# Modulation weights issued together, small loads moved to the GpSimd queue, and the first tile's modulation moved to ScalarE in a hybrid layer kernel

## The chip, the cores and the metric

The kernel runs on one core of one Trainium2 chip. The metric is the device time of one execution in microseconds. The engines are PE (TensorE), DVE (VectorE), ACT (ScalarE), POOL (GpSimd) and SP (SyncE); each has its own program, and they wait for each other through semaphores. Transfers are issued from the queue of SP, ACT or POOL, and 16 DMA engines carry them out.

## The reference

One layer over 256 tokens of width 1024, all in f32, and a final norm:

```
mod = silu(c) @ w_ada + b_ada          # six vectors of 1024
h   = rms_norm(x, g_norm1) * (1 + sc1) + sh1
z   = h @ w_in + b_in                  # 5376 columns: u, v, q, k, v, gates A and B
A   = gmlp_spatial(gelu(u), gelu(v))   # uses w_spatial, b_spatial
B   = sliding-window attention(q, k, v) with rotary (positions) and sinks
x   = x + gt1 * ((sig(gA) * (A @ w_o_a) + sig(gB) * (B @ w_o_b)) @ w_out)
x   = x + gt2 * MoE(rms_norm(x, g_norm2) * (1 + sc2) + sh2)   # top 4 of 32 experts
out = rms_norm(x, g_final)
```

## The kernel before, in words

The tokens are two tiles of 128 (t = 0, 1). The weights of the dense part come in 17 blocks of up to 512 columns (v0, v1, u0, u1, q0, q1, kv, ga0, ga1, gb0, gb1, then oa, ob, out in two each), those of the modulation in 12 blocks of 512 columns (ada0 to ada11). A block of either kind has 2 MB. Four buffers hold them: ring 0 to 2 hold ada1, ada2 and ada3 first and then the dense blocks in turn, ring 3 holds ada0 and then ada4 to ada11. A load waits until the block before it in its buffer has been used (`item_used`, in `load` at L385).

A dense block is computed in three passes of eight matmuls for each tile (`rows_times`, L1242). Both operands are split in an upper part (a cast to fp32r, L741) and a lower part (the difference). The passes are lower h and upper h times the upper weights, and upper h times the lower weights. The upper part of the weights is made by DVE (`w_parts_upper`, L743), the lower part half by DVE (`w_parts_lower`, L751) and half by POOL (L505); both are line L329 in the profile. The third pass of a tile waits for both halves. The parts of h are made by `x_parts` (L762, L765) for each tile.

A modulation block is one group of 16 matmuls on a replicated silu(c) (`ada`, L1269, matmuls L1277), a copy by ACT (`part_copy`, L536, L547), and four small products that add the quarters (`ada_rows`, L1281, L1288). ada0 to ada3 are needed for h: their results and b_ada are added (L810), transposed (L1319) and give the columns `mod_col` and `mul1` (L813, L815). ada4 to ada11 are spread between the dense blocks.

The order of the work is written out by hand, one program for each engine; nothing else decides it.

- SP (L379): c, x; then it waits for ACT's small loads (`cond_in`, L383); ada0 to ada3 (L402); v0, after ada1 is used, and its bias; the small loads w_spatial, b_spatial, positions, four of sinks, w_router, b_router (L407 to L416) and four of b_ada (L417, issued at L375); ada4, v1, u0, and from there one modulation block, one dense block and one bias at a time. After the dense part the weights of the experts, in 20 slots.
- ACT (L530): the small loads g_norm1 and four of b_ada; silu(c) (L554); the squares of x (L558), a square root (L561), the copies of ada0 to ada3; h of tile 1 (L571); then the loads of the layer norm's gain and bias (L577) and the gelus (L583).
- DVE (L730): the replicated silu(c), the inverse root (L777 to L785), the normalised x (L806); L810 to L815; h of tile 0 (L823); x_parts of tile 0, w_parts_upper of v0, x_parts of tile 1, w_parts_lower of v0, then v1.
- POOL (L482): constants until L497; it waits for w_spatial and b_spatial (L500), clears the masked part of w_spatial (L501), and then makes its half of each block's lower part in turn (L505).
- PE (L1217): 16 transposes of the normalised x (L1309), ada0 to ada3 (L1314), the transposes of the modulation (L1319), v0 of both tiles, ada4, the transposes of w_spatial (L1336), v1 and so on (L1321).

DVE waits for positions and sinks (L859) after the bias of v0, and for the rest of b_ada (L873) before the bias of v1. The experts' part (L1540 to L1641) goes through 32 experts with blocks of 32 tokens; its gate and up products are L1592, its down products L1627.

The lines of the pass that the steps speak of are

```
for n, (lhsT, w) in enumerate(((up, w_upper[i % 2]), (low, w_upper[i % 2]), (up, w_lower[i % RING]))):
    if n == 2:
        pe.wait_ge(ev("w_lower_dve"), i + 1)
        pe.wait_ge(ev("w_lower_pool"), i + 1)
```

Of the kernel before, what the change touches and what calls it, by code (L numbers as in the profile page):

```python
# [11 lines left out]
ALU = mybir.AluOpType  # L12
ACT = mybir.ActivationFunctionType
AX = mybir.AxisListType

P = 128
# [45 lines left out]
def bass_hybrid_layer(nc, x, c, positions, w_ada, b_ada, g_norm1, w_in, b_in, ln_v_g, ln_v_b,  # L62
# [47 lines left out]
    with ctx:  # L110
# [269 lines left out]
        def _(sp):  # L380
            sp.dma_start(c_col, c[0].rearrange("(k p) -> p k", p=P)).then_inc(c_in, 16)
            sp.dma_start(x_sb[:, :, :], x[0].rearrange("(t p) d -> p t d", p=P)).then_inc(x_in, 16)
            sp.wait_ge(cond_in, 80)  # L383

            def load(name, w, used=None):  # L385
                if used:
                    item_used(sp, used)
                slot = ring_slot(name)[0]
                sp.dma_start(ring[slot][:, :, 0:w.shape[1]],
                             w.rearrange("(k p) n -> p k n", p=P)).then_inc(ring_in[slot], 16)  # L390

            def load_ada(j, used=None):
                load(f"ada{j}", w_ada[0, :, j * COLS:(j + 1) * COLS], used)
# [8 lines left out]
            for j in range(4):  # L402
                load_ada(j)
            load(*dense[0][:2], "ada1")
            load_bias(0)

            sp.dma_start(ws, w_spatial[0].rearrange("h i j -> i h j")).then_inc(gmlp_in, 16)  # L407
            sp.dma_start(bs, b_spatial[0].rearrange("h i -> i h")).then_inc(gmlp_in, 16)
            sp.dma_start(pos_i[:, :], positions[0].rearrange("(t p) -> p t", p=P)).then_inc(attn_in, 16)
            for hh in range(2):  # L410
                for r in range(2):
                    sp.dma_start(sk[hh * CH:(hh + 1) * CH, r, :],
                                  sinks[0:1, :].rearrange("a (g m) -> a m g", m=4)[:, 2 * hh + r, :].to_broadcast([CH, 4]))\
                       .then_inc(attn_in, 16)
            sp.dma_start(wr, w_router[0].rearrange("(k p) e -> p k e", p=P)).then_inc(route_in, 16)
            sp.dma_start(br, b_router[0:1, :].to_broadcast([P, E])).then_inc(route_in, 16)  # L416
            load_b_ada(sp, 4, 12, b_ada_in)  # L417
            load_ada(4, "ada0")
# [64 lines left out]
        def _(pool):  # L483
# [15 lines left out]

            pool.wait_ge(gmlp_in, 32)  # L500
# [30 lines left out]
        def _(act):  # L531
# [34 lines left out]
            for h in range(2):  # L566
                name = f"xT1{h}"
                bank = z_wait(act, name)
                for i in range(4):
                    k = 4 * h + i  # L570
                    last = act.activation(hT[:, k, P:2 * P], bank[:, i * P:(i + 1) * P], ACT.Identity,  # L571
                                          bias=mod_col[:, 0, k:k + 1], scale=mul1[:, k:k + 1])
                z_done(last, name)
# [157 lines left out]
        def _(dve):  # L731
# [85 lines left out]
            dve.wait_ge(ev("mod_col_ready"), 2)  # L817
            for h in range(2):
                name = f"xT0{h}"
                bank = z_wait(dve, name)  # L820
                for i in range(4):
                    k = 4 * h + i
                    last = dve.tensor_scalar(hT[:, k, 0:P], bank[:, i * P:(i + 1) * P], mul1[:, k:k + 1],  # L823
                                             mod_col[:, 0, k:k + 1], ALU.mult, ALU.add)
                z_done(last, name)
            for t in range(TILES):
                for h in range(2):
                    z_gone(dve, f"xT{t}{h}")
                x_parts(hT, upper_a, hT_lower, "hT_parts", slice(t * P, (t + 1) * P))
                if t == 0:  # L830
                    w_parts_upper(0)
            w_parts_lower(0)
# [833 lines left out]
```

## Time and profile before

| | |
|---|---|
| median of 3 runs | 1365.93 us (1364.82 to 1366.85) |
| the profiled execution's own time | 1366.62 us |
| its span in the profile | 1364.6 us |
| PE, DVE, ACT, POOL busy | 80%, 31%, 16%, 9% |
| mean granted clock of PE | 0.878 of 2.4 GHz |
| moved by DMA | 473.22 MB, mean 347 GB/s |

The profile shows one execution. Busy times are of the engines' own instructions; SP and the queues (SPq, ACTq, POOLq) show how long issuing a transfer took, which is not how long the transfer lasted. L12 is line 12 of the kernel. A line can be a helper's: L389 issues every weight block, L741 every cast to an upper part, L329 every lower part of weights. "idle before" is the time that the engine stood still just before an instruction, and behind the arrow is what ended it.

### The profile page before, as it was taken

What the parts mean: (1) busy time and instruction counts of PE and PEld (TensorE: products, weight loads), DVE (VectorE), ACT (ScalarE), POOL (GpSimd) and SP (SyncE); (2) the same over time, 40 slices, a digit from 0 to 9 for tenths busy, and PEclk for the clock granted to TensorE, in tenths of its full rate; (3) what the DMA queues carried; (4) which work ended last, traced back from release to release, by engine and by line L of the source; (5) the groups of instructions that cost most, each with busy time, mean ns of one, the idle gap of its engine ahead of it and who ended that gap; (6) DMA issues with size and microseconds to landing.
All of it is one profiled execution on the core that took longest, in us unless ns stands there. A gap on an engine that the chain in (4) does not pass through costs nothing.

```text
span 1364.6 us, 26032 instructions
## 1 busy us (share of the span) xinstructions
PE 1096.6 (80%) x10234; PEld 508.0 (37%) x10235; DVE 425.8 (31%) x990; ACT 222.4 (16%) x428; POOL 117.9 (9%) x46
## 2 busy tenths in 40 slices
PE   3689999986997668756899989998667687967874
PEld 1457677864332223111343434343211133311322
DVE  1487687965221112111222222222111122211214
ACT  2112123023211011000111212121100011100112
POOL 0154344510000000000000000000000000000001
PEclk9699999985997779768899989999787788977978
DMA  8786965629999999999869999829999996999991
GB/s 308 249 318 234 356 231 177 218 88 384 416 416 416 415 417 418 417 417 416 366 252 417 418 392 371 367 107 418 416 418 417 418 393 264 417 417 416 415 416 44
DMA packets 113244, 473.22 MB, mean 347 GB/s; under 512 B 12784, under 2 KB 16496, under 8 KB 80272
## 3 DMA queue, kind: packets, MB, share of 16 engines
q1 hardware_dynamic: 110880, 469.03, 86.0%
q10 hardware_dynamic: 2288, 3.02, 0.8%
q8 instruction: 67, 1.10, 0.3%
q14 instruction: 9, 0.07, 0.0%
HBM read 470.98 MB, written 1.05 MB: 346 GB/s over the span
## 4 chain that ended last, share of the span: by engine, by line
PE 36%; SPq 26%; DMA 26%; DVE 5%; issue 5%; ACT 1%; POOL 0%; ACTq 0%; DVEq 0%
PE bank L1592 13%; SPq L360 12%; SPq L354 11%; DMA gate_up<-in_w_down_dram 10%; DMA gate_up<-in_w_gate_up_dram 9%; PE bank L1255 9%; PE bank L1627 6%; DMA down<-in_w_down_dram 3%; DVE gate_up_r L741 2%; PE bank L1558 2%; PE bank L1544 2%; DMA gate_up<-in_w_in_dram 1%; DMA gate_up<-in_w_o_b_dram 1%; DMA gate_up<-in_w_ada_dram 1%; PE bank L1277 1%
## 5 line engine op out<-in xcount | busy, mean ns | idle before, releaser
L1592 PE MATMUL bank<-gate_up,mod 128*32 128x512 f32 x2592 | 362.2, 684 | 118.1 <-DMA gate_up<-in_w_gate_up_dram 73.4
L1186 DVE TENSOR_SCALAR front<-bank 128x256 f32<-128x256 f32 x50 | 21.2, 424 | 709.4 <-PE bank L1592 709.4
L1592 PEld LDWEIGHTS bank<-gate_up,mod 128*32 128x32 f32 x2592 | 78.9, 118 | 332.9 <-issue 165.9
L1627 PE MATMUL bank<-gate_up,mod 128*32 128x256 f32 x2496 | 152.6, 389 | 35.2 <-DMA gate_up<-in_w_down_dram 31.2
L1255 PE MATMUL bank<-gate_up_r 128*128 128x512 f32 (+1 forms) x544 | 138.2, 401 | 20.1 <-DVE gate_up_r L741 11.3
L1255 PEld LDWEIGHTS bank<-gate_up_r 128*128 128x128 f32 x544 | 101.7, 194 | 49.2 <-issue 20.8
L329 POOL TENSOR_TENSOR gate_up_r<-gate_up,gate_up_r 128x2048 fp32r<-128x2048 f32 (+1 forms) x17 | 108.8, 6398 | 128.3 <-DVE gate_up_r L741 128.3
L1592 PE MATMUL bank<-down,mod 128*32 128x512 f32 x608 | 91.3, 716 | 27.5 <-DMA down<-in_w_gate_up_dram 25.2
L1627 PEld LDWEIGHTS bank<-gate_up,mod 128*32 128x32 f32 x2496 | 75.2, 111 | 101.0 <-DMA gate_up<-in_w_down_dram 46.1
L712 ACT ACTIVATE front<-front 128x256 f32<-128x256 f32 x50 | 20.8, 416 | 537.7 <-DVE front L1186 537.7
L526 POOL TENSOR_TENSOR gate_up<-x_sb,gate_up 128x1024 f32<-128x1024 f32 x2 | 4.7, 2352 | 1038.2 <-DVE x_sb L1209 1038.2
L1558 PE MATMUL bank<-front 32*128 32x256 f32 x816 | 67.7, 452 | 0.5 <-ACT front L724 0.5
L1255 PE MATMUL bank<-gate_up_r,down_r 128*128 128x512 f32 (+1 forms) x272 | 67.5, 391 | 0.0
L712 ACT ACT_TABLE_LOAD x50 | 64.2, 1283 | 1.4 <-issue 0.5
L1558 PEld LDWEIGHTS bank<-front 32*128 32x128 f32 x816 | 42.3, 213 | 55.3 <-issue 51.8
L1544 PE MATMUL bank<-h,front 128*32 128x256 f32 x816 | 57.5, 401 | 1.3 <-DVE front L1130 1.3
L724 ACT ACTIVATE front<-bank 128x256 f32<-128x256 f32 x50 | 19.2, 384 | 225.9 <-PE bank L1627 225.9
L1255 PEld LDWEIGHTS bank<-gate_up_r,down_r 128*128 128x128 f32 x272 | 51.9, 194 | 11.1
L1627 PE MATMUL bank<-down,mod 128*32 128x256 f32 x704 | 42.8, 387 | 13.1 <-DMA down<-in_w_down_dram 12.3
L1592 PEld LDWEIGHTS bank<-down,mod 128*32 128x32 f32 x608 | 17.9, 119 | 87.4 <-DMA down<-in_w_gate_up_dram 59.6
L741 DVE CAST gate_up_r<-gate_up 128x4096 fp32r<-128x4096 f32 (+1 forms) x17 | 43.0, 2530 | 15.9 <-DMA gate_up<-in_w_in_dram 15.7
L1125 DVE TENSOR_SCALAR front<-front 128x2 f32 (+1 forms) x101 | 23.0, 229 | 76.5 <-issue 75.3
(254 smaller groups left out, 829.2 us busy)
## 6 DMA issues: line engine op xcount, KB each, us to landing
gate_up<-in_w_gate_up_dram SPq DMA_DIRECT2D x204, 1024.0 KB, 20.8
gate_up<-in_w_down_dram SPq DMA_DIRECT2D x104, 1024.0 KB, 23.1
down<-in_w_gate_up_dram SPq DMA_DIRECT2D x52, 1024.0 KB, 20.9
gate_up<-in_w_ada_dram SPq DMA_DIRECT2D x12, 2048.0 KB, 9.0
down<-in_w_down_dram SPq DMA_DIRECT2D x24, 1024.0 KB, 24.6
gate_up<-in_w_in_dram SPq DMA_DIRECT2D x10, 2048.0 KB, 14.5
gate_up<-in_w_o_a_dram SPq DMA_DIRECT2D x2, 2048.0 KB, 7.7
gate_up<-in_w_o_b_dram SPq DMA_DIRECT2D x2, 2048.0 KB, 10.5
```

Of the source, the lines that this page charges most:

```text
L329: return eng.tensor_tensor(w_lower[i % RING][:, chunks, 0:cols], ring[i % RING][:, chunks, 0:cols], w_upper[i % 2][:, chunks, 0:cols], ALU ...
L354: eng.dma_start(store(at % SLOTS), w_gu_view[:, bass.ds(e, 1), k, :].rearrange("p a n -> p (a n)"))\
L360: eng.dma_start(store(at % SLOTS).rearrange("p (a n) -> p a n", a=2), w_dn_view[:, bass.ds(e, 1), 2 * i:2 * i + 2, :].rearrange("p a k n - ...
L712: act.activation(g_sig, g_cap, ACT.Sigmoid, scale=ALPHA).then_inc(ev("sig_ready"), 1)
L741: return dve.tensor_copy(dst, src)
L1125: return dve.tensor_scalar(slots, slots_gates[:, bass.ds(e, 1), 0:2].rearrange("p a t -> p (a t)"), slot_base[:, bass.ds(g, 1)], None, ALU ...
L1186: dve.tensor_scalar(g_cap, banks[4][:, 0:HW], LIMIT, None, ALU.min).then_inc(ev("g_ready"), 1)
L1255: last = pe.matmul(bank[:, 0:cols], lhsT[:, k, rows], w[:, k, 0:cols], start=(n == 0 and k == 0), stop=(n == 2 and k == KC - 1))
L1544: last = pe.matmul(banks[6][q * BM:(q + 1) * BM, 0:HW], sel[:, t, :], h2[:, t, q * HW:(q + 1) * HW], start=(t == 0), stop=(t == 1), skip_g ...
L1558: last = pe.matmul(banks[q][:, t * HW:(t + 1) * HW], gT[rows, t * P:(t + 1) * P], y_sb[rows, :], start=False, stop=True, skip_group_check= ...
L1592: last = pe.matmul(banks[4][q * BM:(q + 1) * BM, :], xT[:, k % KG, k // KG, :], w[:, :, q * HW:(q + 1) * HW], start=(k == 0), stop=(k == K ...
L1627: last = pe.matmul(banks[7][q * BM:(q + 1) * BM, 0:HW], hidT[:, k % KG, k // KG, :], w[:, k % 2, q * HW:(q + 1) * HW], start=(k == 0), sto ...
```

## The change

SP issues x after ada0 and ada1, and ada2 and ada3 behind it; its wait for ACT's small loads is gone. The small loads L407 to L417 go from SP's queue to POOL's, which issues them after its constants, with w_spatial, b_spatial and b_ada first. SP's ada4 comes ahead of v0's bias. ACT makes h of both tiles; DVE makes the upper part of v0's weights meanwhile, and the lower part between the parts of tile 0 and those of tile 1.

```diff
@@ sync
             sp.dma_start(c_col, c[0].rearrange("(k p) -> p k", p=P)).then_inc(c_in, 16)
-            sp.dma_start(x_sb[:, :, :], x[0].rearrange("(t p) d -> p t d", p=P)).then_inc(x_in, 16)
-            sp.wait_ge(cond_in, 80)
...
-            for j in range(4):
+            for j in range(2):
+                load_ada(j)
+            sp.dma_start(x_sb[:, :, :], x[0].rearrange("(t p) d -> p t d", p=P)).then_inc(x_in, 16)
+            for j in range(2, 4):
                 load_ada(j)
             load(*dense[0][:2], "ada1")
+            load_ada(4, "ada0")
             load_bias(0)
-
-            sp.dma_start(ws, w_spatial[0].rearrange("h i j -> i h j")).then_inc(gmlp_in, 16)
-            sp.dma_start(bs, b_spatial[0].rearrange("h i -> i h")).then_inc(gmlp_in, 16)
-            sp.dma_start(pos_i[:, :], positions[0].rearrange("(t p) -> p t", p=P)).then_inc(attn_in, 16)
-            for hh in range(2):
-                for r in range(2):
-                    sp.dma_start(sk[hh * CH:(hh + 1) * CH, r, :],
...
-            sp.dma_start(wr, w_router[0].rearrange("(k p) e -> p k e", p=P)).then_inc(route_in, 16)
-            sp.dma_start(br, b_router[0:1, :].to_broadcast([P, E])).then_inc(route_in, 16)
-            load_b_ada(sp, 4, 12, b_ada_in)
-            load_ada(4, "ada0")
             load(*dense[1][:2], "ada2")
@@ gpsimd, behind the constants
+            pool.dma_start(ws, w_spatial[0].rearrange("h i j -> i h j")).then_inc(gmlp_in, 16)
+            pool.dma_start(bs, b_spatial[0].rearrange("h i -> i h")).then_inc(gmlp_in, 16)
+            load_b_ada(pool, 4, 12, b_ada_in)
+            pool.dma_start(pos_i[:, :], positions[0].rearrange("(t p) -> p t", p=P)).then_inc(attn_in, 16)
+            for hh in range(2):
+                for r in range(2):
+                    pool.dma_start(sk[hh * CH:(hh + 1) * CH, r, :],
...
+            pool.dma_start(wr, w_router[0].rearrange("(k p) e -> p k e", p=P)).then_inc(route_in, 16)
+            pool.dma_start(br, b_router[0:1, :].to_broadcast([P, E])).then_inc(route_in, 16)
+
             pool.wait_ge(gmlp_in, 32)
@@ scalar
-            for h in range(2):
-                name = f"xT1{h}"
...
-                    last = act.activation(hT[:, k, P:2 * P], bank[:, i * P:(i + 1) * P], ACT.Identity,
...
+            for t in range(TILES):
+                for h in range(2):
+                    name = f"xT{t}{h}"
...
+                        last = act.activation(hT[:, k, t * P:(t + 1) * P], bank[:, i * P:(i + 1) * P], ACT.Identity,
...
@@ vector
-            dve.wait_ge(ev("mod_col_ready"), 2)
-            for h in range(2):
-                name = f"xT0{h}"
...
-                    last = dve.tensor_scalar(hT[:, k, 0:P], bank[:, i * P:(i + 1) * P], mul1[:, k:k + 1],
...
+            w_parts_upper(0)
             for t in range(TILES):
                 for h in range(2):
                     z_gone(dve, f"xT{t}{h}")
                 x_parts(hT, upper_a, hT_lower, "hT_parts", slice(t * P, (t + 1) * P))
                 if t == 0:
-                    w_parts_upper(0)
-            w_parts_lower(0)
+                    w_parts_lower(0)
             w_parts_upper(1)
             w_parts_lower(1)
```

## Rows read from the trace of the kernel before

**Rows 1.** By stage: length, busy PE, PEld, DVE, ACT, POOL; clock, DMA share, GB/s.

```profile
78.35:155.00 76.65, 76.32 (x448) 55.64 (x448) 54.10 (x73) 12.88 (x21) 33.49 (x6) 1.00 0.78 275
```

**Rows 2.** The chain of waits up to 90 us: start, us, what.

```profile
54.04 15.11 DMA gate_up<-in_w_in_dram
```

**Rows 3.** SP's timeline (start, us, group): the small loads' first, second and last group.

```profile
29.18 0.44 SPq L407 DMA_DIRECT2D gate_up<-in_w_spatial_dram  x1
29.66 7.61 SPq L408 DMA_DIRECT2D sm<-in_b_spatial_dram  x1
...
44.99 8.51 SPq L375 DMA_DIRECT2D mod<-in_b_ada_dram  x4
```

**Rows 4.** PE's timeline from v0 on; in brackets idle before, and what ended it.

```profile
47.65 3.75 PE L1255 MATMUL bank<-gate_up_r 128*128 128x512 f32 x8 [7.57 <-DVE gate_up_r L741]
...
55.87 5.53 PE L1255 MATMUL bank<-gate_up_r 128*128 128x512 f32 x16 [2.03 <-DVE gate_up_r L329]
...
66.81 1.09 PE L1336 MATMUL bank<-ident,gate_up 128*128 128x128 f32 x8
71.61 2.52 PE L1255 MATMUL bank<-gate_up_r 128*128 128x512 f32 x8 [3.70 <-DVE gate_up_r L741]
...
78.35 2.08 PE L1255 MATMUL bank<-gate_up_r 128*128 128x512 f32 x8 [1.25 <-POOL gate_up_r L329]
...
80.71 2.12 PE L1255 MATMUL bank<-gate_up_r 128*128 128x512 f32 x8
...
86.38 1.92 PE L1277 MATMUL bank<-gate_up,crep 128*32 128x512 f32 x16
```

**Rows 5.** PE's timeline until the modulation is done.

```profile
18.07 2.07 PE L1277 MATMUL bank<-gate_up,crep 128*32 128x512 f32 x16
...
20.87 0.43 PE L1288 MATMUL bank<-gate_up,quarter_head 128*32 128x128 f32 x8 [0.73 <-ACT gate_up L547]
...
27.65 2.69 PE L1277 MATMUL bank<-gate_up,crep 128*32 128x512 f32 x16 [2.35 <-DMA gate_up<-in_w_ada_dram]
...
33.07 3.64 PE L1277 MATMUL bank<-gate_up,crep 128*32 128x512 f32 x16 [1.37 <-DMA gate_up<-in_w_ada_dram]
...
37.43 0.66 PE L1288 MATMUL bank<-gate_up,quarter_head 128*32 128x128 f32 x8 [0.72 <-ACT gate_up L547]
```

**Rows 6.** ACT's timeline at the first square of x.

```profile
8.21 1.06 ACT L558 ACTIVATE down<-x_sb 128x1024 f32<-128x1024 f32 x1 [3.03 <-DMA x_sb<-in_x_dram]
```

**Rows 7.** Two stretches of the modulation, columns as in rows 1.

```profile
24.00:28.50 4.50, 1.43 (x20) 0.44 (x20) 0.00 (x0) 0.60 (x1) 0.00 (x0) 1.00 1.05 386
28.50:38.20 9.70, 6.80 (x44) 1.13 (x36) 0.00 (x0) 1.19 (x2) 0.00 (x0) 0.51 1.05 385
```

**Rows 8.** ACT's DMA queue (q10) from 2 to 8.5 us: packets, MB, share of 16 engines.

```profile
q10 hardware_dynamic: 1616, 0.27, 26.3%
```

**Rows 9.** DVE's timeline from the modulation columns on.

```profile
40.40 0.17 DVE L815 SCALAR_TENSOR_TENSOR sm<-sm 128x8 f32<-128x8 f32 x1
...
43.35 0.69 DVE L741 CAST gate_up_r<-down 128x1024 fp32r<-128x1024 f32 x1
...
45.22 2.29 DVE L741 CAST gate_up_r<-gate_up 128x4096 fp32r<-128x4096 f32 x1
...
48.14 5.47 DVE L765 TENSOR_TENSOR down_r<-down,gate_up_r 128x1024 fp32r<-128x1024 f32 x1
53.53 2.28 DVE L329 TENSOR_TENSOR gate_up_r<-gate_up,gate_up_r 128x2048 fp32r<-128x2048 f32 x1
```

**Rows 10.** Groups of instructions up to 78 us: busy us, mean ns, idle before.

```profile
L571 ACT ACTIVATE down<-bank,sm 128x128 f32<-128x128 f32 x8 | 2.9, 467 | 3.2 <-DVE sm L815 3.2
```

**Rows 11.** POOL's timeline: its wait for the small loads, and v1's half.

```profile
42.56 0.52 POOL L501 MEMSET gate_up<- 64x512 f32 x1 [39.16 <-DMA sm<-in_b_spatial_dram]
...
71.54 6.67 POOL L329 TENSOR_TENSOR gate_up_r<-gate_up,gate_up_r 128x2048 fp32r<-128x2048 f32 x1 [19.01 <-DVE gate_up_r L741]
```

**Rows 12.** The page's DMA issues: count, KB each, median us to landing.

```profile
gate_up<-in_w_o_a_dram SPq DMA_DIRECT2D x2, 2048.0 KB, 7.7
```

More of the change, by code:

```diff
@@ L401, in load_bias @@
                                  dense[i][2].to_broadcast([P, cols])).then_inc(bias_in[i % 2], 16)
-            for j in range(4):
+            for j in range(2):
+                load_ada(j)
+            sp.dma_start(x_sb[:, :, :], x[0].rearrange("(t p) d -> p t d", p=P)).then_inc(x_in, 16)
+            for j in range(2, 4):
                 load_ada(j)
             load(*dense[0][:2], "ada1")
+            load_ada(4, "ada0")
             load_bias(0)
-            sp.dma_start(ws, w_spatial[0].rearrange("h i j -> i h j")).then_inc(gmlp_in, 16)
-            sp.dma_start(bs, b_spatial[0].rearrange("h i -> i h")).then_inc(gmlp_in, 16)
-            sp.dma_start(pos_i[:, :], positions[0].rearrange("(t p) -> p t", p=P)).then_inc(attn_in, 16)
-            for hh in range(2):
-                for r in range(2):
-                    sp.dma_start(sk[hh * CH:(hh + 1) * CH, r, :],
-                                  sinks[0:1, :].rearrange("a (g m) -> a m g", m=4)[:, 2 * hh + r, :].to_broadcast([CH, 4]))\
-                       .then_inc(attn_in, 16)
-            sp.dma_start(wr, w_router[0].rearrange("(k p) e -> p k e", p=P)).then_inc(route_in, 16)
-            sp.dma_start(br, b_router[0:1, :].to_broadcast([P, E])).then_inc(route_in, 16)
-            load_b_ada(sp, 4, 12, b_ada_in)
-            load_ada(4, "ada0")
             load(*dense[1][:2], "ada2")
@@ L498, in _ @@
                                pattern=[[-QR, NQT], [0, P]], channel_multiplier=1).then_inc(ev("consts"), 1)
+            pool.dma_start(ws, w_spatial[0].rearrange("h i j -> i h j")).then_inc(gmlp_in, 16)
[5 more added lines that the diff above has]
+                    pool.dma_start(sk[hh * CH:(hh + 1) * CH, r, :],
+                                   sinks[0:1, :].rearrange("a (g m) -> a m g", m=4)[:, 2 * hh + r, :].to_broadcast([CH, 4]))\
+                        .then_inc(attn_in, 16)
+            pool.dma_start(wr, w_router[0].rearrange("(k p) e -> p k e", p=P)).then_inc(route_in, 16)
+            pool.dma_start(br, b_router[0:1, :].to_broadcast([P, E])).then_inc(route_in, 16)
             pool.wait_ge(gmlp_in, 32)
@@ L565, in _ @@
             act.wait_ge(ev("mod_col_ready"), 2)
-            for h in range(2):
-                name = f"xT1{h}"
-                bank = z_wait(act, name)
-                for i in range(4):
-                    k = 4 * h + i
-                    last = act.activation(hT[:, k, P:2 * P], bank[:, i * P:(i + 1) * P], ACT.Identity,
-                                          bias=mod_col[:, 0, k:k + 1], scale=mul1[:, k:k + 1])
-                z_done(last, name)
+            for t in range(TILES):
+                for h in range(2):
+                    name = f"xT{t}{h}"
+                    bank = z_wait(act, name)
+                    for i in range(4):
+                        k = 4 * h + i
+                        last = act.activation(hT[:, k, t * P:(t + 1) * P], bank[:, i * P:(i + 1) * P], ACT.Identity,
+                                              bias=mod_col[:, 0, k:k + 1], scale=mul1[:, k:k + 1])
+                    z_done(last, name)
             for t in range(TILES):
@@ L816, in _ @@
                .then_inc(ev("mod_col_ready"), 2)
-            dve.wait_ge(ev("mod_col_ready"), 2)
-            for h in range(2):
-                name = f"xT0{h}"
-                bank = z_wait(dve, name)
-                for i in range(4):
-                    k = 4 * h + i
-                    last = dve.tensor_scalar(hT[:, k, 0:P], bank[:, i * P:(i + 1) * P], mul1[:, k:k + 1],
-                                             mod_col[:, 0, k:k + 1], ALU.mult, ALU.add)
-                z_done(last, name)
+            w_parts_upper(0)
             for t in range(TILES):
```

## The prediction

> **What bounds the kernel now.** The page shows no single bound, so I read the busy time by stage, then the chain of waits of the front, and last each engine's timeline there. From 78 to 155 us PE is busy 76.3 of 76.7 us [rows 1]. What comes after is fixed by data, each load waiting for the use of the buffer before it, so I take all behind 78 us to shift as one block. The change is then read at one event: the start of v1's third pass for tile 0, at 78.35 us now. From there PE runs without a break.
>
> The chain up to it ends in the load of v1, issued at 54.04 and landed at 69.17 [rows 2]. SP could not issue it earlier: it was busy with the twelve small loads from 29.18 to 53.50 us, end to end [rows 3]. PE's timeline shows the price: idle 2.0 us in v0 (for DVE's L329), 3.7 before v1 (for its cast) and 1.25 in it (for POOL) [rows 4]. These 7.0 us can be won behind v0's first matmul, and what matmuls lose after a gap: v1's first pass took 2.52 us, 2.12 the next time.
>
> Ahead of v0 the modulation loads bound. PE waits for ada2 and ada3, which come in 5.42 us apart (27.65, 33.07) [rows 5].
>
> **The change part by part.**
>
> *x behind two modulation loads.* x, now the first large load, has landed at 8.21 us, when ACT's square starts [rows 6]. With ada0 and ada1 ahead of it, 5.42 us each, it lands at 19.1 us at the earliest. This matters, since PE's program has the 16 transposes of the normalised x ahead of ada0: nothing of the modulation is computed before x is there. Early weights gain nothing by themselves.
>
> *The POOL queue's packets.* They now run beside the critical ones. I count 5,504 for the twelve moved loads from their shapes: 1,024 each for w_spatial, b_spatial, the four of b_ada together, the four of sinks and w_router, 256 for positions and 128 for b_router. ACT's small loads had 1,616 packets, for 26.3% of 6.5 us: 1.7 us of all engines [rows 8]; 5,504 would be 5.8 us. How many go ahead of x no row shows: from none (x at 19.1) to all (24.9). No row is nearer to one end, so I take half: x at 22.0.
>
> *To the modulation columns.* From x landed to ada0's matmuls 9.86 us (8.21 to 18.07): squares, root, normalisation, transposes [rows 5, 6]. Then four steps. The last weights land at 30 to 36 us (8.21 and four times 5.42, and the packets) and are used at 41.6, so the steps run back to back: 2.80 from the matmuls to the start of L1288 (18.07 to 20.87) and 0.43, 3.23 each, 12.9 together. From the last L1288's end to L815's end 2.48 (38.09 to 40.57) [rows 5, 9]. Sum: 22.0 + 9.9 + 12.9 + 2.5 = 47.3 us, against 40.6 now: **6.7 us later**. This needs the high clock. The granted clock is 1.00 (2.4 GHz) from 24 to 28.5 us, and 0.51 (near 1.2 GHz) from 28.5 to 38.2; the fall follows a stretch in which PE was busy 1.43 of 4.5 us [rows 7]. Ada0's 16 matmuls took 2.07 us, ada3's 3.64 [rows 5]. Now PE would be busy 2.5 of each 3.23 us, so I expect no fall.
>
> *hT by ACT, DVE at the weights.* Now ACT makes tile 1 and DVE tile 0 side by side; DVE then casts and subtracts tile 0 (1.9 us, 43.35 to 45.22) and casts v0 (2.29), and PE starts at 47.65, 7.1 us after the columns [rows 4, 9]. In the new order DVE casts v0 first while ACT makes tile 0 (2.9 us for eight [rows 10]); tile 1 costs ACT as much again, beside DVE's work. But the cast releases POOL's half of v0's subtraction, and DVE and POOL take turns: beside POOL's half DVE's L765 took 5.47 us, where cast and subtraction together had taken 1.9, and POOL's L329 took 6.67 beside DVE's, which takes 2.28 [rows 9, 11]. So POOL, 4.4 us alone, runs from 2.4 to 6.8 us after the columns, DVE's 1.9 us on hT only then, and PE starts at 8.7 instead of 7.1: **1.6 us lost** where the step was meant to gain.
>
> *The load of v1.* Without the small loads SP issues v0 when ada1 is used, at 37.2 us. A 2 MB load into a free queue lands after 7.7 us [rows 12], at 44.9; DVE wants it at 47.3. ada4, the bias and v1 follow by 56.4; DVE wants v1 at 60.3. Both are covered, by 2.4 and 3.9 us.
>
> *PE from there.* Passes 1 and 2 of v0 6.2 us (47.65 to 53.84); then from the unbroken stretch 1.9 for the third pass, 5.7 for tile 1 (80.71 to 86.38), 1.9 for ada4, 1.1 for L1336 and 3.8 for two passes of v1 [rows 4]: 20.5 us without a wait. DVE has v0's halves ready 11 us after the columns, DVE and POOL v1's by 22; PE asks at 14.9 and 29.2. **Sum:** 47.3 + 8.7 + 20.5 = 76.5 against 78.35, **1.9 us won**. Before it was 40.6 + 7.1 + 30.7. So 10.2 us of idle time and slow matmuls go, and 6.7 and 1.6 come back.
>
> *POOL's twelve issues.* No row shows an issue on POOL. On SP the twelve took 24.3 us, one of them 7.61, one 0.44 [rows 3]; at these two prices each they would take 5.3 and 91. POOL is free from 3.4 us (42.56 less its 39.16 of waiting) [rows 11]; with SP's prices it is done at 27.7, 22 us before its first subtraction. I take that, as the same loads are the nearest rows. The Trainium skill, "DMA: Bandwidth & Descriptors", section "SWDGE vs HWDGE vs iDMA", says that GpSimd's descriptors are computed by software and SP's and ACT's by hardware, and the page gives about 1 us to the first byte against 0.6. An estimate by that ratio makes 40.5 us of issues, done at 43.9, and leaves the sum as it is; no row here shows it.
>
> The loads from POOL have other users: w_spatial's mask, needed by PE at about 73 us; positions and sinks, for DVE behind v0's bias at about 70; the rest of b_ada before v1's bias. At 27.7 us all are early. What POOL's issues delay first is its half of v0.
>
> **Against the runs.** The profiled execution took 1366.6 us, the median of the runs is 1365.93, 0.7 us less. So 1364.7 for it and **1364.0** for the median. With x at either end the gain is 4.8 or -1.0 us: 1361.1 to 1366.9. A measurement can tell 0.2% here, 2.7 us.
>
> **The rivals.**
>
> *A. POOL issues until 50 to 54 us: 1360.2.* Then DVE comes first: hT is cast and subtracted 4.9 us after the columns, PE starts at 52.2, POOL's half is ready before 58.4, and 3.8 us more are won, 5.7 in all. For it: twice SP's price is plausible. Against: the window is narrow.
>
> *B. Slower: POOL still issues when PE wants its half.* The place is POOL's first L329. PE starts as in A and wants it at 58.4, with 5.7 us in hand; the half takes 4.4, so the sign turns when the issues end at 59.7, and beyond it each us costs one. That is 56.3 us for twelve, 4.7 each against SP's mean 2.0. At three times SP's sum (end at 76.3) the loss is 16.6 us: 1382.5. For it: 5,504 packets, most of 4 to 512 bytes, and no row for POOL. Against: SP's issues waited in part for a full queue, so their price alone is lower. The Trainium skill, "SBUF — State Buffer", section "SBUF: two separate sides", says that a two-port DVE instruction keeps GpSimd from writing descriptors. By that page DVE's work before ada0 would be added to POOL's issues: at most the 14.7 us between 3.4 and 18.07, an end at 42.4, so alone it decides nothing.
>
> *C. Slower: the modulation runs at the low clock.* Then each of the four steps takes 3.64 + 0.72 + 0.66 = 5.0 us, 7.2 more in all, and 5.3 us are lost: 1371.2. For it: PE now stands idle until 28 us. Against: ada0's matmuls came behind the same transposes and ran in 2.07 us [rows 5].
>
> *D. The change doesn't do what it says*: x isn't held back by the weights ahead of it. If it shared the engines with ada0 alone it would land at 13.6 us, the columns would be there at 38.9 instead of 47.3, still behind all weights, and 10.3 us were won: 1355.6. Against: ada2 and ada3, on one queue, landed strictly one after the other [rows 5].
>
> **Chances.** Forecast case 0.55, of which 0.38 within 0.2%, 0.14 faster and 0.03 slower (its own range 1361 to 1367); A 0.15, B 0.14, C 0.10, D 0.06. B and C are slower but for 0.02 within 0.2%. Faster 0.14 + 0.15 + 0.06 = 0.35; slower 0.03 + 0.22 = 0.25; same 0.38 + 0.02 = 0.40. The range goes from A (1360.2, with 0.7 for the spread of the runs) to C's 1371.2, as 1359.5 to 1371.5; outside are most of B and D.
>
> **What would show it.** Right: ACT's first square at 19 to 25 us; the four L1277 groups at 1.9 to 2.1 us each without a DMA wait; L815 near 47; the first L1255 near 56, after POOL's L329; the third pass of v1 near 76.5 with PE unbroken from v0; no SP issues from 24 to 37 us. Wrong if: POOL's last issue ends after 50 us; x lands before 19 us; PE's clock is 0.5 during the modulation; PE waits for v1 or u0 all the same; or the stretches behind 78 us change their lengths by over 2 us.

## The result and the profile after

The changed kernel takes 1378.83 us, the median of 4 runs (1377.42 to 1380.06), beside 1365.66 for the kernel before: a ratio of 1.0100 as recorded, 95% interval 1.0084 to 1.0115 (the quotient of these two medians is 1.0096). It is **1% slower**, 14.8 us above the forecast and 7.3 above the range. The profiled execution has a span of 1378.1 us, 13.5 more than before.

The small loads that change queues are thirteen, not twelve as the prediction and the expectations have it: w_spatial, b_spatial, positions, four of sinks, w_router, b_router and four of b_ada.

The timeline of the front, all engines (start, us, group; in brackets the idle time before and what ended it):

```profile
3.35 1.11 POOL L489 DMA_DIRECT2D gate_up<-in_w_spatial_dram  x1
...
11.13 20.23 SPq L387 DMA_DIRECT2D gate_up<-in_w_ada_dram  x2
...
11.71 0.59 POOL L499 DMA_DIRECT2D sm<-in_b_router_dram  x1
...
35.38 1.06 ACT L559 ACTIVATE down<-x_sb 128x1024 f32<-128x1024 f32 x1 [30.29 <-DMA x_sb<-in_x_dram]
...
45.24 2.79 PE L1270 MATMUL bank<-gate_up,crep 128*32 128x512 f32 x16
...
57.34 0.43 PE L1281 MATMUL bank<-gate_up,quarter_head 128*32 128x128 f32 x8 [0.72 <-ACT gate_up L548]
...
59.62 0.17 DVE L817 SCALAR_TENSOR_TENSOR sm<-sm 128x8 f32<-128x8 f32 x1
...
62.08 4.50 POOL L329 TENSOR_TENSOR gate_up_r<-gate_up,gate_up_r 128x2048 fp32r<-128x2048 f32 x1 [48.38 <-DVE gate_up_r L743]
62.83 4.30 DVE L743 CAST gate_up_r<-down 128x1024 fp32r<-128x1024 f32 x1 [0.83 <-ACT down L573]
...
67.16 1.22 DVE L767 TENSOR_TENSOR down_r<-down,gate_up_r 128x1024 fp32r<-128x1024 f32 x1
...
68.44 3.78 PE L1248 MATMUL bank<-gate_up_r 128*128 128x512 f32 x8 [9.14 <-DVE down_r L767]
...
88.73 1.98 PE L1248 MATMUL bank<-gate_up_r 128*128 128x512 f32 x8
```

The row to see is ACT's: x has landed at 35.38 us, where it had landed at 8.21 [rows 6]. Everything behind hangs on it. PE has 16 transposes of x ahead of ada0, so its first ada0 matmul comes at 45.24 (18.07 before, [rows 5]), the columns at 59.8 instead of 40.6 [rows 9], v0 at 68.44 instead of 47.65, and v1's third pass at 88.73 instead of 78.35 [rows 4]. From there on the stage is the old one:

Three stretches of after: from v1's third pass on, from the logits to the first expert, and the experts (length, busy PE, PEld, DVE, ACT, POOL; clock, DMA share, GB/s).

```profile
88.73:165.40 76.67, 76.18 (x449) 55.55 (x447) 48.10 (x71) 13.10 (x21) 30.68 (x6) 1.00 0.81 288
327.43:360.69 33.26, 27.78 (x162) 15.38 (x166) 13.03 (x62) 10.23 (x13) 0.00 (x0) 0.60 1.02 414
360.69:1378.10 1017.41, 802.60 (x8640) 296.12 (x8632) 199.31 (x667) 145.04 (x256) 4.69 (x2) 0.87 0.92 376
```

The first stands against [rows 1]: 76.67 us and 76.65. The logits' first matmul comes 10.9 us later than before (327.43 against 316.57). So 10.9 of the 13.5 us are lost in the front. The other two stretches took 34.63 and 1013.40 us before: 1.4 us are won and 4.0 lost, so 2.6 more are lost, the 4.0 of them some 290 us and more behind the last changed line's work. These splits come from one execution of each kernel. Two later kernels with the same front (h1 and h2, below) have the logits at 324.4 and 324.5 us, so the front's loss is 8 to 11 us.

The page of after, DMA queues (packets, MB, share of 16 engines):

```profile
q1 hardware_dynamic: 105168, 467.83, 84.8%
q10 hardware_dynamic: 2288, 3.02, 0.8%
q0 software_dynamic: 608, 1.21, 0.7%
q8 instruction: 67, 1.10, 0.3%
q14 instruction: 34, 0.28, 0.1%
```

q1 is SP's queue, q10 ACT's, q0 is new and POOL's. q14, which carries instructions, had 9 packets before and has 34; what that means is told with h1 to h3.

What delayed x, in the DMA queues of three windows of after: 3 to 35.4 us (q1, q0), 14 to 20 (q0, q1), and 24 to 35.4 (q1).

```profile
q1 hardware_dynamic: 3409, 7.32, 64.9%
q0 software_dynamic: 608, 1.21, 27.7%
...
q0 software_dynamic: 217, 0.23, 51.2%
q1 hardware_dynamic: 217, 0.41, 31.3%
...
q1 hardware_dynamic: 1872, 4.28, 97.1%
```

From 14 to 20 us the engines carry one packet of q0 for each of q1: 217 and 217. Those of q0 take 51.2% of 96 engine microseconds, 0.23 us each; the q1 stream, 0.387 MB/us when alone (2 MB in 5.42 us), falls to 0.07. The Trainium skill, "DMA: Bandwidth & Descriptors", section "Queues, rings and completion order", says that each DMA engine goes round between the queues that have work, a whole packet at a time; the equal counts agree. Over the front q0's 608 packets take 27.7% of 32.4 us, 9.0 us of all engines. And q1 had moved 7.32 MB when x was complete, though x ends at 5.24 MB of its queue (two blocks and 1 MB). The engines were out of step: some were at ada2 and ada3 while the slowest still owed its part of x. 2.08 MB at 0.387 are 5.4 us. 9.0 and 5.4 are 14.4 of the 15.9 us by which x was later than in e1, below.

This is an account, not the whole mechanism. For some microseconds the engines did not even work at their full share (columns as in rows 1):

```profile
17.00:18.00 1.00, 0.00 (x0) 0.00 (x0) 0.00 (x0) 0.00 (x0) 0.00 (x0) 1.00 0.48 33
18.00:19.00 1.00, 0.00 (x0) 0.00 (x0) 0.00 (x0) 0.00 (x0) 0.00 (x0) 1.00 0.71 17
19.00:20.00 1.00, 0.00 (x0) 0.00 (x0) 0.00 (x0) 0.00 (x0) 0.00 (x0) 1.00 0.45 52
```

From 17 to 20 us they were busy 48, 71 and 45% and moved 33, 17 and 52 GB/s, although x was still owed. From 18 to 19 us 11 packets of q0 took 65.4% of the 16 engines' time, almost the whole microsecond each. Why the idle engines were not at q1's stream no run shows; SP stood in its issue of ada2 and ada3 at that time (11.13 to 31.36 us).

### The profile page after: what moved, and what is told of

Its sections match the earlier page's. It is cut to its first block, busy times and chain, and to the rows that moved or that the text cites. A ratio compares the mean times of both kernels' runs of the same rounds, so it can differ in the third digit from the quotient of the medians.

```text
span 1378.1 us, 26031 instructions
## 1 busy us (share of the span) xinstructions
PE 1087.2 (79%) x10234; PEld 504.6 (37%) x10235; DVE 418.9 (30%) x982; ACT 225.5 (16%) x436; POOL 126.5 (9%) x59
## 3 DMA queue, kind: packets, MB, share of 16 engines
q1 hardware_dynamic: 105168, 467.83, 84.8%
q10 hardware_dynamic: 2288, 3.02, 0.8%
HBM read 470.98 MB, written 1.05 MB: 343 GB/s over the span
## 4 chain that ended last, share of the span: by engine, by line
PE 37%; DMA 27%; SPq 22%; issue 7%; DVE 5%; ACT 2%; ACTq 0%; DVEq 0%
PE bank L1585 13%; DMA gate_up<-in_w_down_dram 11%; SPq L360 10%; PE bank L1248 10%; SPq L354 10%; DMA gate_up<-in_w_gate_up_dram 9%; PE bank L1620 6%; DMA down<-in_w_down_dram 4%; DMA x_sb<-in_x_dram 2%; DVE gate_up_r L743 2%; PE bank L1551 1%; PE bank L1537 1%; PE bank L1270 1%; DMA gate_up<-in_w_o_b_dram 1%; SPq L349 1%
## 5 line engine op out<-in xcount | busy, mean ns | idle before, releaser
L1620 PE MATMUL bank<-gate_up,mod 128*32 128x256 f32 x2496 | 153.7, 390 | 40.3 <-DMA gate_up<-in_w_down_dram 36.5
L1620 PEld LDWEIGHTS bank<-gate_up,mod 128*32 128x32 f32 x2496 | 75.0, 111 | 106.7 <-DMA gate_up<-in_w_down_dram 52.5
L714 ACT ACT_TABLE_LOAD x50 | 64.2, 1283 | 1.5 <-issue 0.5
L1248 PEld LDWEIGHTS bank<-gate_up_r,down_r 128*128 128x128 f32 x272 | 51.6, 194 | 10.9
L1118 DVE TENSOR_SCALAR front<-front 128x2 f32 (+1 forms) x101 | 23.0, 228 | 76.5 <-issue 75.3
## 6 DMA issues: line engine op xcount, KB each, us to landing
gate_up<-in_w_o_b_dram SPq DMA_DIRECT2D x2, 2048.0 KB, 10.5
```

Of the source, the lines that this page charges most:

```text
L714: act.activation(g_sig, g_cap, ACT.Sigmoid, scale=ALPHA).then_inc(ev("sig_ready"), 1)
L1118: return dve.tensor_scalar(slots, slots_gates[:, bass.ds(e, 1), 0:2].rearrange("p a t -> p (a t)"), slot_base[:, bass.ds(g, 1)], None, ALU ...
L1248: last = pe.matmul(bank[:, 0:cols], lhsT[:, k, rows], w[:, k, 0:cols], start=(n == 0 and k == 0), stop=(n == 2 and k == KC - 1))
L1620: last = pe.matmul(banks[7][q * BM:(q + 1) * BM, 0:HW], hidT[:, k % KG, k // KG, :], w[:, k % 2, q * HW:(q + 1) * HW], start=(k == 0), sto ...
```

## The experiments

Theory L: the packets of POOL's queue delay x, and all else follows as forecast. Its rival X: x would be late anyway behind two blocks, or something else holds the front. (The expectations of e1 and e2 call L "theory P" and the rival Q; in those of g1 to g4 P is another theory, told there.) The table has, in us, x landed, the columns ready, v0's first matmul, v1's third pass, the logits' first matmul, the time from there to the end of the span; then q14's packets, the place of SP's loop in its program (the number of its first instruction; what it is for is told with h1 to h3), the median and its ratio to before with its 95% interval. All times but the last two columns are from one profiled execution of each kernel: after, h1 and h2 have the same front, and x landed at 35.4, 34.1 and 33.9, so a difference of 1.5 us in x, or of 3 us at the logits, says nothing.

| kernel | x | columns | v0 | v1, 3rd | logits | to end | q14 | loop | median | ratio |
|---|---|---|---|---|---|---|---|---|---|---|
| before | 8.2 | 40.6 | 47.7 | 78.4 | 316.6 | 1048.0 | 9 | 84 | 1365.66 | |
| after | 35.4 | 59.8 | 68.4 | 88.7 | 327.4 | 1050.7 | 34 | 71 | 1378.83 | 1.0100 [1.0084, 1.0115] |
| e1 | 19.5 | 44.2 | 49.2 | 86.2 | 325.6 | 1048.4 | 8 | 84 | 1374.3 | 1.0063 [1.0046, 1.0080] |
| e2 | 19.4 | 52.5 | 61.1 | 80.0 | 318.0 | 1053.2 | 34 | 71 | 1373.13 | 1.0065 [1.0048, 1.0081] |
| e3 | 25.0 | 49.5 | 58.1 | 81.5 | 321.3 | 1054.9 | 33 | 76 | 1374.77 | 1.0069 [1.0052, 1.0085] |
| e4 | 28.2 | 51.7 | 56.8 | 84.3 | 322.7 | 1051.4 | 33 | 79 | 1376.91 | 1.0088 [1.0072, 1.0105] |
| e5 | 8.6 | 51.7 | 60.5 | 80.4 | 318.9 | 1051.2 | 34 | 71 | 1371.29 | 1.0055 [1.0038, 1.0071] |
| e6 | 8.3 | 40.0 | 49.5 | 76.9 | 316.6 | 1048.2 | 9 | 84 | 1365.33 | 1.0005 [0.9990, 1.0021] |
| f1 | 8.1 | 38.0 | 45.1 | 68.8 | 307.3 | 1050.0 | 35 | 71 | 1360.14 | 0.9972 [0.9962, 0.9983] |
| f2 | 8.2 | 36.9 | 42.0 | 64.3 | 308.1 | 1051.2 | 34 | 71 | 1361.54 | 0.9978 [0.9965, 0.9991] |
| g1 | 8.2 | 35.7 | 42.8 | 64.9 | 306.1 | 1050.9 | 34 | 71 | 1359.94 | 0.9968 [0.9958, 0.9978] |
| g2 | 8.0 | 40.3 | 47.4 | 77.6 | 316.3 | 1046.5 | 9 | 82 | 1365.07 | 1.0006 [0.9989, 1.0023] |
| g3 | 8.1 | 37.2 | 44.3 | 66.4 | 314.2 | 1047.0 | 9 | 84 | 1363.82 | 0.9996 [0.9983, 1.0009] |
| g4 | 8.0 | 37.0 | 42.0 | 62.6 | 310.2 | 1050.5 | 33 | 71 | 1363.62 | 0.9994 [0.9984, 1.0004] |
| h1 | 34.1 | 57.5 | 66.2 | 85.9 | 324.4 | 1048.2 | 9 | 84 | 1375.3 | 1.0082 [1.0064, 1.0100] |
| h2 | 33.9 | 57.5 | 66.1 | 86.0 | 324.5 | 1050.2 | 34 | 78 | 1378.07 | 1.0103 [1.0085, 1.0121] |
| h3 | 8.0 | 38.0 | 45.1 | 68.8 | 307.1 | 1046.1 | 9 | 84 | 1355.97 | 0.9941 [0.9920, 0.9962] |

**e1: the small loads back on SP**, behind v0's bias, the rest as changed.

```diff
@@ sync, behind load_bias(0); the same lines are taken from gpsimd
+            sp.dma_start(ws, w_spatial[0].rearrange("h i j -> i h j")).then_inc(gmlp_in, 16)
...
+            sp.dma_start(br, b_router[0:1, :].to_broadcast([P, E])).then_inc(route_in, 16)
```

> The changed kernel with its twelve small loads back on SP's queue, behind v0's bias; x stays behind ada0 and ada1, and the new order of hT stays. Theory P (POOL's packets hold x back): x lands at 19 to 20 us instead of 35.4, the modulation columns are there at 43.6, PE starts v0 near 52; SP's small loads then delay v1 again, issued at 55 to 60 us, so the third pass of v1 comes at 78 to 84 and the time is 1366 to 1372 us. Rival Q (the SP queue itself holds x back: its issue took 8.4 us behind two weight blocks, and POOL has no part in it): x lands at 33 us or later and the time is 1377 us or more.

x lands at 19.52 us. That is the 19.1 of two blocks in a row, so L stands and X falls: the two blocks cost 11.3 us, the other 15.9 are POOL's packets. But the gain goes again, and the third pass (78 to 84 expected) and the time (1366 to 1372) both came out later than I had expected: SP issues the small loads from 37.7 to 59.3 us, and POOL, which stands at its wait for b_spatial, can't touch v0's half until 55.86, and v1 is late as well. The line of POOL's timeline:

```profile
55.86 0.52 POOL L502 MEMSET gate_up<- 64x512 f32 x1 [52.47 <-DMA sm<-in_b_spatial_dram]
```

**e2: POOL waits for x** before it issues.

```diff
+            pool.wait_ge(x_in, 16)
             pool.dma_start(ws, w_spatial[0].rearrange("h i j -> i h j")).then_inc(gmlp_in, 16)
```

> The changed kernel, POOL issues its small loads only after x has landed. Theory P: x at 19 to 20 us; POOL's packets then run beside ada2 and ada3. If they cost these what they cost x, ada3 lands near 44, the columns are there at 49 and the time is 1365; if little, columns at 43.6 and 1360. Rival Q: x at 33 us or later, 1377 or more.

x lands at 19.38, but the packets now meet ada2 and ada3 (PE's timeline):

```profile
44.97 3.64 PE L1271 MATMUL bank<-gate_up,crep 128*32 128x512 f32 x16 [6.48 <-DMA gate_up<-in_w_ada_dram]
```

ada3 comes where I had it if the packets cost it what they had cost x (45.0, expected 44), but the time is 8 us above the 1365 expected for that.

**e3 and e4: which of the thirteen.** e3 gives positions and sinks to SP and leaves eight on POOL; e4 leaves those five alone on POOL and gives SP the eight.

```diff
@@ e3: sync (e4: the other eight loads instead)
+            sp.dma_start(pos_i[:, :], positions[0].rearrange("(t p) -> p t", p=P)).then_inc(attn_in, 16)
+            for hh in range(2):
...
```

> The changed kernel with positions and the four loads of sinks on SP behind v0's bias; w_spatial, b_spatial, b_ada, w_router and b_router stay on POOL. Theory P1 (among POOL's packets it is those of the sinks, single 4-byte elements, that block the engines from 16 to 24 us): x lands at 22 to 25 us, 1362 to 1367. Rival P2 (all of POOL's packets cost alike, by bytes or by packets): x lands at 30 us or later, 1373 or more.

> The other half: only positions and sinks on POOL, the rest on SP behind v0's bias. P1: x at 27 us or later. P2: x at 20 to 22 us. The time says less here, since SP's loads delay v1 as well: 1368 to 1378 by P1, 1365 to 1370 by P2.

Against e1's 19.5 the eight delay x by 5.5 us, the five by 8.6, and all thirteen by 15.9. The five move 5 KB: what counts isn't bytes. Nor is it the number of packets: 160 of the 608 are theirs. The trace gives 4 bytes as the size of the elements that they write; b_spatial, one of the eight, is of that kind too, and no run moves it alone. So x came as P1 had it in both, and e4's time too (1376.9, 1368 to 1378 expected), but not e3's (1374.8, 1362 to 1367 expected).

**e5: x first**, the rest as changed.

```diff
+            sp.dma_start(x_sb[:, :, :], x[0].rearrange("(t p) d -> p t d", p=P)).then_inc(x_in, 16)
             def load(name, w, used=None):
```

> The changed kernel with x issued ahead of ada0 again, its one edit; POOL still issues its loads from 3.4 us on. What e1 to e4 left open is whether x's place costs anything of its own, or whether POOL's packets merely delay whichever load is last. Theory L (POOL's packets cost the queue beside them some 16 us, whatever stands there): x lands at 9 to 13 us, but ada3 lands at 43 to 46 (the last of the 9.4 MB landed at 45 in the changed kernel), PE waits for it, the columns are there at 49 to 52 and the third pass of v1 comes at 78 to 82: 1365 to 1372 us. Rival X (only x's place matters): the columns at 37 to 40, the third pass near 68, 1355 to 1358.

x lands at 8.6, and ada0, now the next in the queue, pays:

```profile
28.80 3.20 PE L1270 MATMUL bank<-gate_up,crep 128*32 128x512 f32 x16 [9.91 <-DMA gate_up<-in_w_ada_dram]
```

ada0's matmuls come 10.7 us later than before (18.07), ada3's 11.9 (44.98 against 33.07). So whatever SP's queue holds is delayed, and x's place chooses what. But x's place has a price of its own, too. The columns are ready at 35.7 to 38.0 us with x first and no packets beside it (f1, g1, g3, h3, below), at 44.2 with x behind two blocks (e1), at 51.7 with the packets (e5) and at 59.8 with both (after): 6 to 9 us for x's place, 13 to 16 for the packets, if after's columns are taken at 57.5 (h1) to 59.8.

**e6: the new order of h alone**, on the kernel before (the scalar and vector parts of the diff).

> The kernel before with only the new order of hT (ACT makes both tiles, DVE casts v0 first and makes its lower part between the tiles). By the reading of turns between DVE and POOL: columns at 40.6 as before, PE starts v0 at 49.2 instead of 47.6, its third pass follows without a wait, v1 still comes at 69.2 and hides both, so the third pass of v1 stays at 78.4 and the time at 1364.3 within 2 us. Rival (ACT helps DVE as intended): PE starts at 45.5.

PE starts v0 9.5 us behind the columns instead of 7.1 (8.6 expected), as DVE and POOL take turns at v0's weights. The end doesn't move (1.0005): 2.4 us lost ahead of v0 lie within what PE idled behind it [rows 4].

**f1: what seemed right to do instead.** The kernel before without SP's wait for the conditions and with ada4 ahead of v0's bias; POOL issues the thirteen only behind its half of v0, at 49.9 us, when nothing urgent is in SP's queue.

```diff
@@ gpsimd, behind the constants
+            pool.wait_ge(ev("w_upper_ready"), 1)
+            lower(pool, 0, slice(KC // 2, KC)).then_inc(ev("w_lower_pool"), 1)
+            pool.dma_start(ws, w_spatial[0].rearrange("h i j -> i h j")).then_inc(gmlp_in, 16)
...
+            pool.dma_start(br, b_router[0:1, :].to_broadcast([P, E])).then_inc(route_in, 16)
```

> The kernel before with SP free of the small loads and of its wait for ACT's, and POOL issuing the twelve only behind its first half of a subtraction (v0's). x first, hT as before. Theory P/L: no packet of POOL runs beside the modulation weights; ada3 lands near 30, columns at 37.4, v1 lands near 47 to 52, PE runs v0 and v1 without a wait for a load; third pass of v1 at 67 to 70: 1353 to 1357 us. If instead POOL's packets hold v1 back by the 16 us, third pass at 75 to 80 and 1360 to 1366.

The first version faster than before. v1's third pass comes 9.5 us earlier, the logits 9.2, yet the median wins 4.3, less than the 7 to 11 expected. 2.0 us of that go behind the logits; the rest is the spread of the runs, as the profiled execution of before (1366.62) was 2.2 us above the median of before beside f1 (1364.43), and f1's own 1.05 below its median. **f2** adds the new order of h, with POOL's half of v0 held until the first parts of h stand (`pool.wait_ge(ev("hT_parts"), 1)`):

> As f1 but with the new order of hT, and POOL's first subtraction waits until DVE has made the parts of hT's tile 0, so that POOL can't take its turn ahead of them. By the reading of turns PE starts v0 5 us after the columns instead of 7.1 or 8.7, and v1's third pass comes 26 us after them: near 63.5, 1349 to 1353 us. If the turns are no matter, it is as f1.

PE starts 5.0 us behind the columns, as expected, and loses it again at a modulation block that POOL's packets delay (3.23 us at 75.66); 1361.54 us stand against 1349 to 1353 expected.

**g1 to g4: who issues.** By then kernels with DMAs of POOL's took 1.6 us or more longer behind the logits than the three without. Theory P: using the software queue costs that. Theory N: it doesn't matter who issues; a kernel that comes to the logits earlier waits longer behind them, and the gain goes. g1 is f1 with the thirteen on ACT, g2 the kernel before with the router's two on POOL, g3 is f1 with the thirteen on SP behind v1's bias, g4 is g1 with f2's order.

```diff
@@ g1: scalar, behind its waits for v0's xT
+            act.dma_start(ws, w_spatial[0].rearrange("h i j -> i h j")).then_inc(gmlp_in, 16)
...
+            load_b_ada(act, 4, 12, b_ada_in)
@@ g2: gpsimd, in its loop over the blocks
+                if i == 0:
+                    pool.dma_start(wr, w_router[0].rearrange("(k p) e -> p k e", p=P)).then_inc(route_in, 16)
+                    pool.dma_start(br, b_router[0:1, :].to_broadcast([P, E])).then_inc(route_in, 16)
```

> The order of f1 (x ahead of everything, the weights of the modulation behind it without a wait, the old order of hT), but the twelve small loads are issued by ACT: ten behind its waits for v0's xT and ahead of its layer norm's loads, the router's two behind the copies of block 4; POOL issues no DMA at all. Theory P (a kernel whose POOL issues any DMA loses some 4 us in the expert stage): v1's third pass at 67 to 71 us as in f1 (68.84), logits at 306 to 309, expert stage 1012 to 1013.5 instead of f1's 1015.3, total 1355 to 1357.5. Theory N (the expert stage doesn't care who issued what 900 us earlier; its 4 us are the earlier phase of the stream against its compute): the same front, the expert stage as in f1, total 1359 to 1361. Price of ACT's twelve issues: if they cost as on SP, ACT is 6 us or more late for v0's gelu, v1's third pass at 73 to 76 and total 1361 to 1364.

> The kernel before, with the router's two small loads alone issued by POOL behind its part of the first operator, where nothing in the front waits for them. The front should stand as before: columns ready at 40.6 us, v1's third pass at 78.4, logits at 316.6. Theory P (any DMA issued by POOL costs the expert stage some 4 us): logits unchanged and the total at 1367 to 1369. Theory N (the expert stage depends on the phase in which it starts, not on POOL's queue): 1363.5 to 1365.5.

> f1 without a DMA of POOL's and without one of ACT's: the twelve small loads stay on SP, now behind v1's bias and ahead of u0. SP's 24 us of issues lie behind everything that v0 and v1 need. Front: columns ready at 38, v0 at 45, v1's third pass at 68 to 72. Theory P: expert stage 1011 to 1013, total 1355 to 1358. Theory N: 1359 to 1361. Rival: SP's 24 us of issues now delay u0 and w_in's later blocks, so that logits come at 312 or later and the total at 1362 or more.

> g1 with the new order of hT and POOL's first operator held until the first half of hT stands, as in f2. In f2 PE began v0 5.0 us after the columns instead of 7.1, but POOL's packets delayed the modulation's sixth block. Without these packets: columns at 37 to 38, v0 at 42 to 43, v1's third pass at 63 to 66, logits at 303 to 306. Theory P: total 1352 to 1356. Theory N: the gain of the front is lost again in the expert stage, total 1359 to 1361.

P falls from both sides: g1 has no q0 and takes 1050.9 us to the end, g2 has q0 and takes 1046.5. N gives the right totals for g1 and g2, but not the whole: g1 and g3 are 8 us apart at the logits and still 3.9 at the end. That an early start costs a part stays possible with these four; g1, f1 and h3, below, settle it: logits at 306.1, 307.3 and 307.1, and 1050.9, 1050.0 and 1046.1 us from there. g3's SP is late with the modulation blocks (PE waits 7.42 us for one at 81.86); in g4 ACT issues until 64.2 us and PE waits 2.72 for its copy, so its logits come at 310.2, where I had expected 303 to 306. But the column q14 parts the kernels without an exception: 8 or 9 packets and at most 1048.4 us to the end, or 33 to 35 and at least 1050.0. And it goes with SP's program: the kernels with the 34 packets have at least five loads fewer on SP ahead of its loop over the experts, whichever queue has them.

**h1 to h3: the place of SP's loop.** The loop has six turns, and in the traces of all kernels SP takes 272 instructions from one jump back to the next. Theory I: where it begins decides whether its instructions have to be fetched again in every turn. h1 is the changed kernel with 13 wait instructions more on SP, all long fulfilled, so that the loop begins where it did before; h2, its control, has 7; h3 is g1 with 13. The edit is that of h1 (two waits of the source make one instruction); h2 has `range(13)`.

```diff
             item_used(sp, "ob1")
+            for _ in range(25):
+                sp.wait_ge(x_in, 16)
             first_loads(ring_slots("ob1"))
```

> The changed kernel with 13 wait instructions more on SP, all long fulfilled (on x), between the front's loads and the first loads of the experts. SP's loop over the experts then begins at its 84th instruction, as in the kernel before, instead of its 71st. Theory I (the place of SP's loop decides whether its code stays loaded or is fetched again in every turn): q14 falls from 34 packets to 8 or 9, SP's stretches of issue of 3.2 us go, the front stays as in the changed kernel (x 35.4, v1's third pass 88.7, logits 327.4), expert stage 1012 to 1015 instead of 1017.3, total 1374.5 to 1377. Theory N (the phase in which the stream meets the compute decides, the fetches are harmless): q14 may fall, the total stays at 1378.8 +- 1.

> The control of h1: only 7 wait instructions more, so that SP's loop begins at its 78th instruction, where it was within one of its place in e4 (79), which still had 33 packets on q14. Theory I: q14 at 33 or 34, total as the changed kernel, 1378.8 +- 1. If the wait instructions themselves changed the time, h2 would show half of what h1 shows.

> g1, the fastest so far (1359.94), with the same 13 wait instructions, SP's loop at its 84th instruction. Theory I: q14 8 or 9 packets, front as g1 (v1's third pass 65.0, logits 306.2), expert stage 1012 to 1014.5 instead of 1017.4, total 1355.5 to 1358. Theory N: 1360 +- 1.

h1 and h2 have the same front within 0.15 us. The windows of the experts' stage, h1 and then h2:

```profile
357.49:1372.60 1015.11, 807.41 (x8640) 297.36 (x8632) 199.41 (x667) 145.05 (x256) 4.69 (x2) 0.87 0.92 377
```

```profile
357.61:1374.70 1017.09, 800.17 (x8640) 295.11 (x8632) 199.42 (x667) 145.02 (x256) 4.70 (x2) 0.88 0.92 376
```

and q14 on the pages of h1 and of h2:

```profile
q14 instruction: 9, 0.07, 0.0%
```

```profile
q14 instruction: 34, 0.28, 0.0%
```

Six more instructions, which do nothing, save 2.0 us in this stage and 2.8 in the medians of six runs each (1375.3, 1374.31 to 1377.4, and 1378.07, 1376.6 to 1380.58). In the chain of waits one sees where, in after around 493 us:

```profile
493.66 0.03 SPq L360
493.69 3.18 issue
496.87 0.39 SPq L360
```

SP stands between two loads for 3.18 us and waits for nothing that the profile shows. There are three such stretches of 3.2 us in the experts' part of after (493.69, 645.79, 999.33), three of 4.1 to 4.3 in h2's, none in h1's or h3's, while in all of them SP feeds a stream that keeps the DMA engines busy 92% of the time.

The larger part stands just ahead of them, in the same chain of after:

```profile
638.71 5.57 issue
645.79 3.24 issue
...
992.26 5.55 issue
999.33 3.22 issue
```

At 638.7 and 992.2 us SP has just jumped back to the start of its loop. In the trace's records of SP's own instructions its next one comes 5.1 to 5.8 us behind each of the five jumps back in all ten kernels with 33 to 35 packets, and 0.2 to 0.3 us behind it in the other seven, with 8 or 9. The packets fall into the same places. From 480 to 505 us, around the first jump (486.6), and from 500 to 1350 us after has on q14

```profile
q14 instruction: 4, 0.03, 0.3%
...
q14 instruction: 22, 0.18, 0.1%
```

and h1 has no packet on q14 from 500 to 1350 us. So five jumps cost SP some 27 us in all; most of it is hidden, as SP issues ahead of the stream, and 2 to 3 us are not.

h3 is **the fastest version**: 1355.97 us (1353.6 to 1359.2), 0.6% under the kernel before. Its stretch from the logits is 4.8 us shorter than g1's, more than h1 against h2; with one profile each, how much of that is the fetches isn't settled. Nor is the spread among the kernels with 33 to 35 packets: from 1050.0 (f1) to 1054.9 us (e3) behind the logits, wider than the effect.

## Why the prediction was wrong

**What held.** The bound, in that the event that I chose (v1's third pass) carried the front's part: 10.4 us there, 10.9 at the logits. From x to ada0's matmuls: 9.86 forecast, 9.86 measured. Four steps of the modulation: 12.9 and 12.5 (45.24 to 57.77), at the granted clock of 1.00, so C did not come true. The last L1281's end to the columns: 2.5 and 2.0. v0 8.7 behind the columns: 8.65, for the reason given: beside POOL's 4.50 us DVE's cast took 4.30 instead of 0.69 [rows 9]. From v0 to v1's third pass 20.5: 20.3, without a wait of PE's, though DVE waited 1.99 us for v1, which the forecast had covered by 3.9. POOL's issues: done at 12.3, sooner than the 27.7 taken and than the 43.9 of the estimate beside it; B fell for that reason, and A with it.

**The step that failed** is "The POOL queue's packets": "5,504 would be 5.8 us", and the choice of half of that, "x at 22.0". x came at 35.4. Had it come at 22.0, v1's third pass would have come at 88.73 - 13.4 = 75.3, beside the 76.5 of the sum: this term is the whole error of the front and 1.2 us more, which the other terms gave back. Three things were wrong in it.

- *The price of a packet.* It was taken from ACT's queue [rows 8]: 26.3% of 6.5 us and 16 engines over 1,616 packets, 17 ns each. POOL's were 608, not 5,504, and took 27.7% of 32.4 us and 16 engines, 236 ns each: 9.0 us together where 5.8 were thought to be the bound. I had tied the price to a count, and neither carries over to a queue of another kind: on SP's and ACT's queues the same loads are 5,712 packets (110,880 less 105,168 on q1; 8,000 less 2,288 on q10 in g1), near my count.
- *The bound.* I took the engines' time that the packets use as the most that x can lose. But a transfer is complete when its slowest engine is, and the engines went out of step by 2.08 MB, 5.4 us.
- *Half.* The packets were all issued by 12.3 us, all ahead of x's last part, and from 14 to 20 us they were carried one for one with q1's: none of them had to wait for x's end. Behind 24 us only 36 were left.

D looked at the opposite error only. No rival had x later than 24.9 us.

**The second error** is "I take all behind 78 us to shift as one block". It was 2.6 us off, and h1 against h2 (2.0 by the profiles, 2.8 by the medians) show that this is the size of what comes from the thirteen loads that left SP's program: the loop behind them begins elsewhere, and at each jump back SP stands for 5.1 to 5.8 us while packets run on q14 (34 in all instead of 9). That these packets carry SP's instructions is read from their times, which are those of SP's jumps; how large the blocks of code are that are kept, and why the 82nd instruction is a good place and the 79th isn't, stays open. The prediction had named this under what would prove it wrong ("change their lengths by over 2 us"), with no mechanism for it.

The miscount of the small loads did no harm to the sum, which takes SP's 24.3 us as a whole. It is in A's and B's prices of one issue: 5.3 and 91 us for twelve would be 5.7 and 99 for thirteen, and B's 4.7 us each 4.3.

By medians the 13.2 us are thus 8 to 11 from x, of which the packets' part is the larger, and 2 to 3 from SP's loop. What the change was good for can be had: SP's queue free of small loads for v0 and v1 was worth 9.2 and 10.5 us to the logits in f1 and g1, where x stayed first.

## What to carry to other kernels

Moving small loads from a queue whose issues are late to another queue frees the issuer, but their packets then run beside the critical stream and not behind it. Ask of each load what stands at that time in the other queue, and issue it when nothing urgent does (f1: 49.9 us instead of 3.35, with x first again, turned +1.0% into -0.3%). The block at the head of a chain should have nothing ahead of it and nothing beside it. And when a change moves the time of a stage that it doesn't touch, compare the instruction queues of the two pages: a loop can cost more only because the code ahead of it has another length, which a few idle instructions can test. It shows at the loop's jump back.

## What the runs showed that I had not expected

- POOL issued the thirteen in 9.1 us (3.35 to 12.3), against 24.3 on SP [rows 3]. Not each of them is cheaper there: w_spatial took 1.11 us on POOL and 0.44 on SP, b_spatial 0.91 and 7.61. On ACT they are not cheap either: in g1 positions took 6.24 us to issue and four sinks 6.59.
- Five loads of 5 KB in all, from POOL, delay SP's stream by 8.6 us (e4).
- 13 fulfilled waits on SP make the changed kernel 0.2% faster and g1 0.3%.
- The clock of the modulation makes 2.3 us of difference between kernels alike until then: ada3's matmuls took 3.64 us in f1, at a granted clock of 0.50, and 1.92 in g1, at 1.00, after the same wait of 2.35 us and 2.8 us of PE's work in the 6.5 us ahead of them in both; the columns came at 38.0 and 35.7. What decides it no run shows.
